# Joined two-block kernel: the start, the seams between stages and the order of the sparse attention rewritten

## The chip, the cores and the metric

One core of one Trainium2 chip. The metric is device microseconds (us) of one launch. The profile comes from one profiled execution.

## The reference, cut to what is computed

One sequence of 512 tokens, model width 1024, float32. Two blocks run one after the other.

```python
def first_block(x, c, ...):
    c_act = jax.nn.silu(c)
    for layer in range(2):
        mod = (c_act @ ada_w[layer] + ada_b[layer])[:, None, :]
        sh_a, sc_a, gt_a, sh_m, sc_m, gt_m = jnp.split(mod, 6, axis=-1)
        h = modulate(rms_norm(x, attn_norm[layer]), sh_a, sc_a)
        # layer 0: differential attention; layer 1: sparse attention
        mix = diff_attention(h, ...) if layer < 1 else nsa_attention(h, ..., *shared)
        x = x + gt_a * mix
        h = modulate(rms_norm(x, mlp_norm[layer]), sh_m, sc_m)
        x = x + gt_m * squared_relu_mlp(h, mlp_w1[layer], mlp_w2[layer])
        if layer == 0:
            h_kv = modulate(rms_norm(x, kv_norm), sh_kv, sc_kv)
            shared = nsa_shared_kv(h_kv, w_kv, cmp_pos, cmp_w1, cmp_w2)
    return rms_norm(x, final_norm)
```

The sparse attention has 16 heads in 4 groups and three branches: attention over 31 compressed keys, over selected blocks of keys, and over a window. Their outputs are weighted by gates and added. With 512 tokens the selection takes every block and the window every earlier key, so both are causal attention with a relative bias. The second block is an mLSTM layer, a dilated window attention layer and a gated addition behind each.

## The kernel before

**Numbers.** Every large product is float32 split in two parts (`hi` on ACT writes the rounded part `wH`, `lo` on DVE the rest `wL`), and `three` (L420) issues three matmuls for it: L422, L423, L424. Activations are split in the same way into `hH` and `hL` (`apply_dve`, `apply_act`; semaphores `h_hi`, `h_lo`). A fp32 matmul that is not split shows as two instructions in the trace (x8 for four of them).

**Weights.** They come in halves of 1 MB in the order of a list. SP's `load_half(n)` waits until half n-2 is split (`w_lo`), and one half feeds 48 matmuls of 512 columns on PE. Besides, rows of the modulation weights (`ada`, 512 KB each) are loaded, and DVE reduces each with the broadcast silu(c) (`ada_sum`, L647). They go through two buffers, `adab`.

**Order.** Each engine runs a list written by hand: `pe_first`, `act_first`, `dve_first`, `sp_first` for layer 0, then `_second` for layer 1's attention and so on. Within an engine everything runs in that order. All waits are semaphores.

**The start.** SP loads c, x, the first 16 ada rows in four pieces, and the first two halves. silu(c) is an exponential on ACT and three DVE steps, one a reciprocal (L1266). Then DVE takes the sums of squares, the 16 reductions, `lo(0)`, `lo(1)` and the eight chunks of `hL`; PE's first tile waits for `h_lo`.

**A seam.** Between stages stands an RMS norm: residual and squares, one or two fp32 matmuls with a constant matrix (`stats_pe`, L512 and L515; `stats_two_pe` ahead of the second block), rstd on ACT (logarithm, exponential), then chunk by chunk `tmp` (DVE L532), `hH` (ACT L568), `hL` (DVE L541). PE's next tile waits for the first `h_lo`.

**The stage of compressed keys.** `cmp_pe` (16 x 2 products of 124 columns) runs twice between tiles 26, 27 and 28. The first waits until ACT has copied the four banks of tile 26, and ACT splits a half of weights ahead of these copies.

**Sparse attention** (`nsa_pe`, `nsa_dve`, `nsa_act`). The work is a list of units, `UNITS`. Block i has 128 queries and (i+1)*128 keys; a unit is one bank: four heads for i=0, two for i=1, one for i=2 and 3. Blocks run in the order 0, 1, 2, 3. For a unit, PE computes scores (L1525 and L1526), DVE adds the bias and takes the maximum (L1626), ACT takes the exponentials (L1730), PE transposes (L1535), ACT copies (L1737), PE multiplies with the values, 65 columns (L1564), and per branch DVE divides, gates and adds (L1639 to L1661). For each block come ahead of its units the scores over compressed keys, 32 matmuls of 32 columns (`c_scores`, L1581 and L1582), with their softmax on DVE and ACT into `sc`, transposes (L1589) and a copy into `ptc`. `tail` turns the block's output (L1599) and splits it for tile 29.

The loop of `nsa_pe`, condensed:

The loop of `nsa_pe`, condensed:

```python
for u in range(-6, UN + 5):
    if u == FIRST[i] - 6: c_scores(i)
    scores(u + 2); values(u - 2); turn(u)
    if u == FIRST[i] - 2: c_turn(i)
    if u == FIRST[i + 1] + 4: tail(i)
```

**Late in the second block** SP writes `vD` to memory, waits, and reads it back in another order (L2947 to L2949), ahead of a load of weights (half `N_K2 + 6`).

## Time and profile before

| | us |
|---|---|
| median of 3 runs | 2116.03 (2113.04 to 2121.13) |
| the profiled execution | 2119.31 |
| its span, first to last instruction | 2117.5 |
| PE busy in the span | 1979.0 (93%) |
| DVE busy | 1173.3 (55%) |
| ACT busy | 847.5 (40%) |
| mean granted TensorE clock | 0.958 |

Busy time is what an engine executed. The granted clock is 1.0 where TensorE runs at 2.4 GHz and 0.5 where it runs at 1.2 GHz, and a mean between them says what share of a stretch ran at which. In a timeline row the first number is the start from the span's beginning, the second the time covered, and the brackets hold the idle time of that engine just before, with what ended it.

### The profile page before, as it was taken

The numbers are of one execution on the slowest core, as the hardware profiler recorded it, in microseconds if no ns is written. First come the engines' busy times: TensorE is split into PE (matmuls) and PEld (weight loads), VectorE is DVE, ScalarE is ACT, GpSimd is POOL, SyncE is SP. The second block draws the span as 40 slices with busy tenths as digits, with TensorE's granted clock in tenths as the row PEclk, the third lists the DMA queues.
The fourth block names the chain that finished last, engine by engine and source line by source line (L and its number), as shares of the span: only waits on it lengthen the run. The fifth ranks groups of instructions, "written<-read, shape, count | busy, mean of one in ns | idle before, by whom it ended". The sixth has DMA issues, their size and how long they took to land.

```text
span 2117.5 us, 24340 instructions
## 1 busy us (share of the span) xinstructions
PE 1979.0 (93%) x9300; PEld 1632.0 (77%) x9300; DVE 1173.3 (55%) x2049; ACT 847.5 (40%) x1319; POOL 0.2 (0%) x4
## 2 busy tenths in 40 slices
PE   1999989999998999889989999999999999999999
PEld 0877667888886887789977888888787877777877
DVE  8557846665657465556545333435663455755554
ACT  3226723232223533356633231323444444657343
POOL 0000000000000000000000000000000000000000
PEclk9999998999999979589999999999999999999999
DMA  9661053546554222000022222222121232232021
GB/s 355 209 208 41 1 198 140 202 177 216 179 198 159 99 80 80 0 1 2 1 85 86 92 90 97 99 99 99 60 100 60 80 125 79 81 120 80 1 90 60
DMA packets 42216, 223.85 MB, mean 106 GB/s; under 512 B 4444, under 2 KB 5212, under 8 KB 23694
## 3 DMA queue, kind: packets, MB, share of 16 engines
q1 hardware_dynamic: 41602, 222.25, 29.5%
q8 instruction: 56, 0.92, 0.2%
q10 hardware_dynamic: 524, 0.41, 0.1%
q14 instruction: 34, 0.28, 0.0%
HBM read 219.45 MB, written 3.19 MB: 105 GB/s over the span
## 4 chain that ended last, share of the span: by engine, by line
PE 82%; DVE 8%; DMA 4%; ACT 4%; issue 2%; SPq 0%; DVEq 0%; ACTq 0%
PE bank L422 22%; PE bank L423 22%; PE bank L424 22%; PE bank L1564 3%; PE bank L1535 2%; DMA raw<-wts_d 2%; PE bank L1525 1%; DMA adab<-ada_d 1%; ACT wH L403 1%; PE bank L1526 1%; PE bank L2736 1%; DVE wL L408 1%; DMA ada<-ada_d 1%; DVE tmp L532 1%; PE bank L741 1%
## 5 line engine op out<-in xcount | busy, mean ns | idle before, releaser
L422 PE MATMUL bank<-hH,wH 128*128 128x512 f32 x1328 | 530.2, 399 | 59.5 <-DVE hL L541 37.0
L423 PE MATMUL bank<-hL,wH 128*128 128x512 f32 x1328 | 524.8, 395 | 0.0
L424 PE MATMUL bank<-hH,wL 128*128 128x512 f32 x1328 | 524.2, 395 | 0.0
L422 PEld LDWEIGHTS bank<-hH,wH 128*128 128x128 f32 x1328 | 254.7, 192 | 120.8 <-issue 59.3
L1006 ACT ACTIVATE wH<-raw 128x2048 fp32r<-128x2048 f32 x64 | 122.7, 1917 | 468.8 <-PE bank L424 468.8
L408 DVE TENSOR_TENSOR wL<-raw,wH 128x2048 fp32r<-128x2048 f32 x76 | 174.0, 2290 | 228.0 <-ACT wH L403 227.7
L423 PEld LDWEIGHTS bank<-hL,wH 128*128 128x128 f32 x1328 | 254.7, 192 | 53.7 <-issue 1.0
L424 PEld LDWEIGHTS bank<-hH,wL 128*128 128x128 f32 x1328 | 254.2, 191 | 54.1
L1050 DVE TENSOR_TENSOR wL<-raw,wH 128x2048 fp32r<-128x2048 f32 x64 | 146.5, 2289 | 225.8 <-ACT wH L1006 225.8
L403 ACT ACTIVATE wH<-raw 128x2048 fp32r<-128x2048 f32 x76 | 145.3, 1911 | 246.8 <-PE bank L424 208.4
L422 PE MATMUL bank<-aH,wH 128*128 128x512 f32 x512 | 199.2, 389 | 0.0
L423 PE MATMUL bank<-aL,wH 128*128 128x512 f32 x512 | 199.2, 389 | 0.0
L424 PE MATMUL bank<-aH,wL 128*128 128x512 f32 x512 | 199.2, 389 | 0.0
L647 DVE CUSTOM_DVE_ANT_0 adab<-adab,cb 128x1024 f32<-128x1024 f32 x96 | 115.4, 1222 | 90.3 <-DMA adab<-ada_d 90.3
L422 PE MATMUL bank<-wH,hH 128*128 128x512 f32 x304 | 126.0, 414 | 2.4 <-ACT kT L1239 1.7
L424 PE MATMUL bank<-wH,hL 128*128 128x512 f32 x304 | 119.9, 395 | 0.0
L423 PE MATMUL bank<-wL,hH 128*128 128x512 f32 x304 | 119.7, 394 | 0.0
L423 PEld LDWEIGHTS bank<-aL,wH 128*128 128x128 f32 x512 | 96.1, 188 | 20.0
L422 PEld LDWEIGHTS bank<-aH,wH 128*128 128x128 f32 x512 | 96.1, 188 | 19.9
L424 PEld LDWEIGHTS bank<-aH,wL 128*128 128x128 f32 x512 | 96.1, 188 | 19.9
L1564 PEld LDWEIGHTS bank<-vB,ptB 128*128 128x128 f32 x640 | 91.1, 208 | 18.2 <-issue 5.7
L1626 DVE CUSTOM_DVE_ANT_0 sB<-bank,bt 128x128 f32<-128x128 f32 (+3 forms) x128 | 59.3, 488 | 77.8 <-PE bank L1526 76.8
(367 smaller groups left out, 2633.4 us busy)
## 6 DMA issues: line engine op xcount, KB each, us to landing
raw<-wts_d SPq DMA_DIRECT2D x140, 1024.0 KB, 4.9
adab<-ada_d SPq DMA_DIRECT2D x96, 512.0 KB, 4.4
ada<-ada_d SPq DMA_DIRECT2D x4, 2048.0 KB, 22.4
bt<-bias_rows SPq DMA_DIRECT2D x1, 4096.0 KB, 13.0
x<-x_d SPq DMA_DIRECT2D x1, 2048.0 KB, 9.8
peF<-ple_d SPq DMA_DIRECT2D x2, 1024.0 KB, 5.6
out_d<-x SPq DMA_DIRECT2D x4, 512.0 KB, 2.7
pF<-p_d SPq DMA_DIRECT2D x2, 512.0 KB, 3.5
```

The costliest lines, as they stand in the source:

```text
L403: act.activation(wH[:, n % 2, :], raw[:, n % 2, :], ACT.Copy).then_inc(w_hi, 1)
L408: dve.tensor_tensor(wL[:, n % 2, :], raw[:, n % 2, :], wH[:, n % 2, :].bitcast(F32), ALU.subtract).then_inc(w_lo, 1)
L422: pe.matmul(o, l[0], r[0], start=start, stop=False)
L423: pe.matmul(o, l[0], r[1], start=False, stop=False)
L424: return pe.matmul(o, l[1], r[0], start=False, stop=stop)
L532: dve.scalar_tensor_tensor(out=tmp[:, nth(p, c) % 3, :], in0=x[:, c, :], scalar=scale(c), in1=rstd[:, :], op0=ALU.mult, op1=ALU.mult).then ...
L647: return dve.tensor_tensor_reduce(slot, slot, sb["cb"][:, :], 1.0, 0.0, ALU.mult, ALU.add, dst)
L1006: act.activation(wH[:, n % 2, :], raw[:, n % 2, :], ACT.Copy).then_inc(w_hi, 1)
L1050: dve.tensor_tensor(wL[:, n % 2, :], raw[:, n % 2, :], wH[:, n % 2, :].bitcast(F32), ALU.subtract).then_inc(w_lo, 1)
L1535: last = pe.transpose(bank[:, 2 + u % 2, j * P:(j + 1) * P], pB[:, u % 2, j * P:(j + 1) * P], ident[:, :])
L1564: last = pe.matmul(o[:, r * (HD + 1):(r + 1) * (HD + 1)], ptB[:, u % 2, part.start + j * P:part.start + (j + 1) * P], vB[:, j, b * GRP + g ...
L1626: dve.tensor_tensor_reduce(sB[:, u % 2, part], bank[:, u % 2, part], sb["bt"][:, 4 * g + r, T - w:T], -SCALE, BIG, ALU.add, ALU.min, nm[:, ...
```

## The change

1. **Start.** SP loads the column parameters first, then c, ada rows 8 to 11, x, rows 0 to 3, halves 0 and 1, rows 12 to 15 and 4 to 7. silu(c) is a sigmoid and one product. The 16 reductions take bias and gain in the same instruction and are made in two parts of eight; after the first part the chunks 0 to 3 of `hH`, `hL` are made. PE works the first four halves in the order (tile 0, half 0), (tile 1, half 0), (tile 0, half 1), (tile 1, half 1), and the halves are stored in that order. The bias table `bt` is loaded later, behind half 4.
2. **ada rows** go through four buffers. Halves 14 and 15 are loaded ahead of the reload of silu(c), and small tables behind halves 16 and 17.
3. **Seams.** `first_chunk` issues the eight matmuls of chunk 0 that need only `hH`, then waits for `h_lo`. It is used at the start, tiles 24 and 47, both MLPs and the gated additions. `fill` issues matmuls of the identity with itself into a bank that the next tile overwrites: 13 behind `stats_pe` of norms 1 to 3, 8 behind `stats_two_pe`, 10 at the start, 3, 5, 12, 9 and 3 around the sparse attention.
4. **Compressed keys.** The first `cmp_pe` waits for two banks only, and ACT copies tile 26 before it splits the next half; in `gelu_act` of the second, the copies come before the next split.
5. **Sparse attention.** Blocks 3 and 0 take turns group by group, then blocks 2 and 1. The first score matmul of block 0 covers 256 columns where the bank allows (the next matmul overwrites what is too much), and the first of each pair over compressed keys covers 160 instead of 32, for which `kcH` is stored twice. Compressed weights lie in two buffers `sc` and are turned in place; `ptc` is gone.
6. **vD** goes to memory and back two halves later.

```diff
+        def first_chunk(pe, b0, w, count):
+            pe.wait_ge(h_hi, count)
+            for m in range(4):
+                pe.matmul(bank[:, b0 + m, :], w(m)[0], hH[:, 0, :], start=True, stop=False)
+                pe.matmul(bank[:, b0 + m, :], w(m)[1], hH[:, 0, :], start=False, stop=False)
+            pe.wait_ge(h_lo, count)
+            for m in range(4):
+                pe.matmul(bank[:, b0 + m, :], w(m)[0], hL[:, 0, :], start=False, stop=False)
...
+                ahead = a in (24, 47) and j == 0
+                if ahead:
+                    first_chunk(pe, 4 * (a % 2), lambda m: wpart(n0 % 2, 0, m * P, P), hbase + 1)
+                for kk in range(1 if ahead else 0, 4):
...
+        def fill(pe, o, n):
+            for _ in range(n):
+                pe.matmul(o[:, 0:P], ident[:, :], ident[:, :], start=True, stop=True)
...
+            if s in (1, 2, 3):
+                fill(pe, bank[:, 4 * (next_a % 2) + 3, :], 13)
...
+        def ada_slot(j):
+            return sb["adab"][:, j % 4, :] if j % 4 < 3 else sb["adac"][:, :]
...
+            sp.dma_start(cols[:, :], d["cols"]).then_inc(cols_in, 16)
             sp.dma_start(sb["cb"][:, :], d["c"].to_broadcast([P, D])).then_inc(cb_back, 16)
-            sp.dma_start(x[:, :, :], d["x"]).then_inc(x_in, 16)
-            for g in range(4):
-                sp.dma_start(sb[f"ada{g // 2}"][:, 4 * (g % 2):4 * (g % 2) + 4, :],
-                             d["ada"][4 * g:4 * g + 4].rearrange("k p n -> p k n")).then_inc(ada_h[g], 16)
-                if g == 3:
-                    sp.wait_ge(ada_h[1], 16)
-                    load_half(sp, 0)
-                    sp.wait_ge(ada_h[2], 16)
-                    load_half(sp, 1)
-            sp.wait_ge(ada_h[3], 16)
+            for e in range(2):
+                for t in (1, 0):
+                    sp.dma_start(sb[f"ada{t}"][:, 4 * e:4 * e + 4, :],
+                                 d["ada"][8 * t + 4 * e:8 * t + 4 * e + 4].rearrange("k p n -> p k n"))\
+                        .then_inc(ada_in[2 * e + 1 - t], 16)
+                    if (e, t) == (0, 1):
+                        sp.dma_start(x[:, :, :], d["x"]).then_inc(x_in, 16)
+                    if (e, t) == (0, 0):
+                        load_half(sp, 0)
+                        load_half(sp, 1)
+            load_half(sp, 2)
             sp.wait_ge(f_row, 2)
             sp.dma_start(fscr, sb["frow"][:, :]).then_inc(f_out, 16)
-            sp.wait_ge(f_out, 16)
-
+            sp.wait_ge(cb_ready, 1)
...
+                if n >= 1:
+                    load_half(sp, n + 2)
                 for k in range(max(3 * n - 1, 0), min(3 * n + 2, 24)):
                     ada_load(sp, 16 + k)
+                if n == 2:
+                    sp.wait_ge(f_out, 16)
+                    sp.wait_ge(ada_pre, 16)
+                    sp.dma_start(sb["bt"][:, :, :], skewed).then_inc(bt_in, 16)
+            load_half(sp, 14)
+            load_half(sp, 15)
             sp.wait_ge(c_saved, 16)
             sp.wait_ge(y_lo, 8)
             sp.dma_start(sb["cb"][:, :], csave.to_broadcast([P, D])).then_inc(cb_back, 16)
+            for n in (16, 17):
+                for k in range(4):
+                    ada_load(sp, 40 + 4 * (n - 16) + k)
+                load_half(sp, n)
...
+            hi(act, 0)
+            act.wait_ge(ada_pre, 8)
+            apply_act(act, 0, lambda c: mod(c), chunks=range(0, 4))
+            hi(act, 1)
...
-            hi(act, 1)
-            act.wait_ge(mod_ready, 2)
-            apply_act(act, 0, lambda c: mod(c))
+            hi(act, 2)
+            act.wait_ge(ada_pre, 16)
+            apply_act(act, 0, lambda c: mod(c), chunks=range(4, KC))
...
             dve.wait_ge(cb_ready, 2)
-            dve.tensor_tensor(cb, cb, ce, ALU.mult).then_inc(cb_ready, 1)
-            dve.wait_ge(cb_ready, 3)
-            sq_dve(dve, 0, range(1, 7))
-            for g in range(4):
-                if g == 3:
-                    dve.wait_ge(par_in, 80)
+            for e in range(2):
+                for t in (1, 0):
+                    if (e, t) == (0, 0):
+                        sq_dve(dve, 0, range(1, 7))
+                    dve.wait_ge(ada_in[2 * e + 1 - t], 16)
+                    for c in range(4 * e, 4 * e + 4):
+                        a = sb[f"ada{t}"][:, c, :]
...
+
+            dve.wait_ge(ada_used, 24)
+            mod_cols(dve, 16, 24, 0)
+            mod_scale(dve, 32, ("mlp_norm", 0))
...
+            pe.wait_ge(w_hi, 1)
+            fill(pe, bank[:, 3, :], 10)
+            for n, (a, j) in enumerate(((0, 0), (1, 0), (0, 1), (1, 1))):
+                if n == 1:
+
+                    pe.wait_ge(f_row, 2)
+                pe.wait_ge(w_lo, n + 1)
+                if n == 0:
+                    first_chunk(pe, 0, lambda m: wpart(0, 0, m * P, P), 1)
...
-                pe.wait_ge(acc_free[0], 4 * 14)
+
+                pe.wait_ge(acc_free[0], 4 * 13 + 2)
...
+        GROUPS = [(i, g) for g in range(GRP) for i in (3, 0)]
+        GROUPS += [(2, 0), (2, 1), (1, 0), (1, 1), (2, 2), (1, 2), (2, 3), (1, 3)]
+        ORDER = (3, 0, 2, 1)
...
+        BEGIN = [FIRST[3, 0] - 6, FIRST[0, 0] - 6, FIRST[2, 0] - 6, FIRST[1, 0] - 10]
+        TURN = [LAST[i] + 5 for i in ORDER]
...
-                pe.wait_ge(ks_lo, i + 1)
+
+                pe.wait_ge(ks_lo, max(i + 1, 2))
                 for n, part, c, b, r in parts(u):
-                    pe.matmul(bank[:, u % 2, part], q_stack(4 * g + r, i), ksH[:, b, g, 0:w], start=True, stop=False)
+                    more = min(part.stop + P, T) if i == 0 else part.stop
+                    pe.matmul(bank[:, u % 2, part.start:more], q_stack(4 * g + r, i),
+                              ksH[:, b, g, 0:more - part.start], start=True, stop=False)
...
+            def c_scores(k):
+                i = ORDER[k]
+                if k == 0:
                     pe.wait_ge(acc_free[1], 4 * 14)
                     pe.wait_ge(acc_free[0], 4 * 15)
+                    fill(pe, bank[:, 0, :], 5)
+                    pe.wait_ge(kc_ev, 1)
...
+                    pe.matmul(bank[:, 6 + hd % 2, (hd // 2) * 32:(hd // 2) * 32 + 160], q_stack(hd, i),
+                              sb["kcH"][:, :, :].rearrange("p r n -> p (r n)")[:, g * 32:g * 32 + 160],
+                              start=True, stop=False)
...
+            def c_turn(k):
+                if k == 0:
+                    fill(pe, bank[:, 3, :], 12)
...
+            def c_copy(k):
+                act.wait_ge(x_t, k + 1)
+                act.activation(comp_flat(k), bank[:, 6, :], ACT.Copy).then_inc(x_pt, 1)
...
-                hi(act, n + 3)
+                if a < 26:
+                    hi(act, n + 3)
...
-                    hi(act, N_B1 + 1)
-                    gelu_act(act, 1, N_B1)
+                    gelu_act(act, 1, N_B1, lambda e: hi(e, N_B1 + 1))
...
+                if j == 0:
+                    first_chunk(pe, 4, lambda m: wpart(n % 2, 0, m * P, P), hbase + 1)
+                for kk in range(1 if j == 0 else 0, 4):
...
-                if n == N_K2 + 6:
+                if n == N_K2 + 8:
```

**PE at the entry of the sparse attention.** In these rows `ident` alone is `fill`, `kcH` and `kcL` are compressed keys, `ksH` and `ksL` the keys of both branches, `qs` queries, `pB` a unit's weights that are turned, `sc` compressed weights. Before:

```order
L1581 MATMUL bank<-kcH,qs_105 128x32
L1582 MATMUL bank<-kcL,qs_105 128x32
L1525 MATMUL bank<-ksH,qs_104 128x128
L1526 MATMUL bank<-ksL,qs_104 128x128
L1525 MATMUL bank<-ksH,qs_104 128x128
L1526 MATMUL bank<-ksL,qs_104 128x128
L1525 MATMUL bank<-ksH,qs_104 128x128
L1526 MATMUL bank<-ksL,qs_104 128x128
L1525 MATMUL bank<-ksH,qs_104 128x128
L1526 MATMUL bank<-ksL,qs_104 128x128
L1589 MATMUL bank<-ident,sc 128x128 x4
```

and after the change:

```order
L1668 MATMUL bank<-kcH,qs_106 128x160
L1671 MATMUL bank<-kcL,qs_106 128x32
L1606 MATMUL bank<-ksH,qs_105 128x512
L1608 MATMUL bank<-ksL,qs_105 128x512
L524 MATMUL bank<-ident 128x128 x12
L1680 MATMUL bank<-ident,sc 128x128 x4
L1606 MATMUL bank<-ksH,qs_105 128x512
L1608 MATMUL bank<-ksL,qs_105 128x512
```

The first units behind the compressed scores are of block 3 (512 columns), where they were of block 0 (128), and twelve `fill` matmuls stand ahead of the first turn. A little later, where block 3 hands over to block 0, the change has (`vB` and `ptB` are values and turned weights)

```order
L1606 MATMUL bank<-ksH,qs_105 128x512
L1608 MATMUL bank<-ksL,qs_105 128x512
L1647 MATMUL bank<-vB,ptB 128x65 x4
L1617 MATMUL bank<-ident,pB 128x128 x4
L1606 MATMUL bank<-ksH,qs_105 128x256
L1608 MATMUL bank<-ksL,qs_105 128x128
```

so units of 512 columns and of four times 128 stand side by side.

**SP at the start**, with the loads of c, x, the first ada rows, the weights and the table `bt`. Before:

```order
L1174 DMA cb<-c_d 128x1024
L1175 DMA x<-x_d 128x4096
L1177 DMA ada_63<-ada_d 128x4x1024 x2
L1177 DMA ada_64<-ada_d 128x4x1024 x2
L665 DMA raw<-wts_d 128x2048 x2
L1186 DMA bias_rows<-frow 16x640
L1190 DMA bt<-bias_rows 128x16x512
```

and after the change:

```order
L1206 DMA cb<-c_d 128x1024
L1209 DMA ada_64<-ada_d 128x4x1024
L1213 DMA x<-x_d 128x4096
L1209 DMA ada_63<-ada_d 128x4x1024
L695 DMA raw<-wts_d 128x2048 x2
L1209 DMA ada_64<-ada_d 128x4x1024
L1209 DMA ada_63<-ada_d 128x4x1024
L695 DMA raw<-wts_d 128x2048
```

The weights stand between the two parts of the ada rows, and `bt` comes eleven rows further down.

## Rows read from the trace of the kernel before

**Rows 1.** The page: granted clock of TensorE in 40 slices, in tenths.
```profile
PEclk9999998999999979589999999999999999999999
```

**Rows 2.** Windows of plain matmuls and of norm 2: us, busy (count) per engine, PEclk, DMA.
```profile
400.00:500.00 100.00, 100.00 (x443) 82.81 (x442) 57.03 (x71) 25.30 (x25) 0.00 (x0) 1.00 0.53 185
684.00:692.00 8.00, 6.64 (x17) 5.26 (x18) 7.86 (x11) 5.78 (x8) 0.00 (x0) 0.57 0.01 2
```

**Rows 3.** Timeline of PE, first matmul of the first tile.
```profile
49.97 0.77 PE L422 MATMUL bank<-hH,wH 128*128 128x512 f32 x1 [23.91 <-DVE hL L541]
```

**Rows 4.** Chain that ended last, 22 to 40 us: start, us, what.
```profile
22.33 13.39 DMA raw<-wts_d
...
35.75 1.92 ACT wH L403
...
37.69 2.29 DVE wL L408
```

**Rows 5.** Timeline of ACT and DVE at the start: x has landed, statistics, rstd.
```profile
11.05 1.67 ACT L495 ACTIVATE tmp<-x 128x512 f32<-128x512 f32 x3 [4.42 <-DMA x<-x_d]
...
15.24 4.67 DVE L503 TENSOR_TENSOR tmp<-tmp 128x512 f32<-128x512 f32 x6
...
24.57 0.63 ACT L522 ACTIVATE rstd<-rstd 128x512 f32<-128x512 f32 x1
```

**Rows 6.** Timeline of PE: idle before the diff attention and at norm 1.
```profile
151.33 0.70 PE L741 MATMUL bank<-kT,qT 64*128 64x128 f32 x4 [3.03 <-DVE nm L811]
...
317.91 2.04 PE L512 MATMUL bank<-tmp,mean 128*128 128x512 f32 x2 [4.14 <-DVE tmp L503]
...
326.04 0.77 PE L422 MATMUL bank<-hH,wH 128*128 128x512 f32 x1 [4.38 <-DVE hL L541]
```

**Rows 7.** Waits of PE, 280 to 330 us: in total, times, longest us.
```profile
PE bank L422 <- DVE wL L408: 3.8, 2, 2.0
```

**Rows 8.** Groups of DVE by line, 290 to 312 us.
```profile
L647 DVE CUSTOM_DVE_ANT_0 adab<-adab,cb 128x1024 f32<-128x1024 f32 x7 | 8.5, 1223 | 6.6 <-DMA adab<-ada_d 6.6
```

**Rows 9.** Chain at norm 2.
```profile
682.47 2.08 DVE tmp L532 x3
```

**Rows 10.** Timeline of PE at norms 2 and 4 and at a gated addition.
```profile
678.62 1.10 PE L512 MATMUL bank<-tmp,mean 128*128 128x512 f32 x2 [2.49 <-DVE tmp L503]
...
685.36 0.77 PE L422 MATMUL bank<-hH,wH 128*128 128x512 f32 x1 [4.38 <-DVE hL L541]
...
1491.71 0.76 PE L422 MATMUL bank<-hH,wH 128*128 128x512 f32 x1 [4.31 <-DVE hL L538]
...
1763.71 0.47 PE L422 MATMUL bank<-hH,wH 128*128 128x512 f32 x1 [1.48 <-DVE hL L538]
```

**Rows 11.** Timeline of PE: first `cmp_pe`, and tile 28 behind the second.
```profile
757.93 0.44 PE L422 MATMUL bank<-fH,wH 128*128 128x124 f32 x1 [4.20 <-issue]
...
816.08 0.80 PE L422 MATMUL bank<-hH,wH 128*128 128x512 f32 x1 [2.52 <-ACT gx L1399]
```

**Rows 12.** Windows in the sparse attention.
```profile
866.00:884.00 18.00, 16.44 (x76) 16.07 (x75) 5.96 (x37) 5.28 (x16) 0.00 (x0) 0.50 0.00 0
1006.00:1071.00 65.00, 63.64 (x501) 58.94 (x500) 35.15 (x108) 42.53 (x73) 0.00 (x0) 1.00 0.00 1
852.70:1079.20 226.50, 204.92 (x1425) 195.17 (x1425) 127.10 (x448) 117.40 (x234) 0.00 (x0) 0.84 0.00 1
```

**Rows 13.** Timeline of PE: pairs of 32 and of 256 columns at the full clock.
```profile
994.05 0.26 PE L1582 MATMUL bank<-kcL,qs 128*128 128x32 f32 x1
994.16 0.26 PE L1581 MATMUL bank<-kcH,qs 128*128 128x32 f32 x1
...
918.04 0.28 PE L1525 MATMUL bank<-ksH,qs 128*128 128x256 f32 x1
918.16 0.28 PE L1526 MATMUL bank<-ksL,qs 128*128 128x256 f32 x1
```

**Rows 14.** Timeline of PE in the second block, where `vD` is moved.
```profile
1887.90 0.77 PE L422 MATMUL bank<-hH,wH 128*128 128x512 f32 x1 [3.98 <-DVE wL L408]
```

More of the change, by code:

```diff
@@ L614, in stats_two_pe @@
             pe.matmul(both, mean, sq_slot2(7), start=False, stop=True).then_inc(stat_mm, 1)
+            fill(pe, bank[:, 7, :], 8)
         def root_act(act, s, bank_, dst, eps):
@@ L989, in mlp_pe @@
                             continue
-                        for kk in range(4):
+                        if (q, j) == (0, 0):
+                            first_chunk(pe, 4 * st, lambda m: wpart(n0 % 2, 0, m * P, P), hbase - KC + 1)
+                        for kk in range(1 if (q, j) == (0, 0) else 0, 4):
                             k = 4 * j + kk
@@ L1393, in cmp_pe, with gelu_act @@
                 last.then_inc(half_used, 1)
-        def gelu_act(act, s, n):
+        def gelu_act(act, s, n, then=None):
             act.wait_ge(half_used, n)
@@ L1401, in gelu_act @@
                                ACT.Copy).then_inc(c_ev, 1)
+            if then:
+                then(act)
             act.wait_ge(c_sq, 4 * s + 4)
@@ L1719, in nsa_dve @@
                     lo(dve, HALF0["b_out"])
-                for i in range(NT):
-                    if u == FIRST[i + 1] + 5:
-                        tail(i)
+                for k in range(NT):
+                    if u == TURN[k] + 1:
+                        tail(k)
         def nsa_act(act):
@@ L1813, in act_second @@
             act.wait_ge(c2_mm, 1)
-            act.activation(sb["kcH"][:, :], bank[:, 4, 0:P], ACT.Copy).then_inc(kc_hi, 1)
+            for r in range(2):
+                act.activation(sb["kcH"][:, r, :], bank[:, 4, 0:P], ACT.Copy).then_inc(kc_hi, 1)
             act.wait_ge(g_mm, 1)
@@ L1912, in pe_second @@
             last.then_inc(g_mm, 1)
+            fill(pe, bank[:, 7, :], 3)
             pe.wait_ge(g_e, 1)
@@ L1921, in pe_second @@
             nsa_pe(pe)
+            fill(pe, bank[:, 0, :], 3)
             pe.wait_ge(y_lo, 8 + 8)
```

325 lines of the change are left out of this document (163 added, 162 removed).

## The prediction, made before the changed kernel had run

> **What bounds the kernel now.** I read the page first. The time table has PE busy in 93% of the span, DVE in 55%, ACT in 40%, and the slices of the granted clock [rows 1] are 9 nearly everywhere and fall to 8 in the seventh and to 7, 9, 5 and 8 in the fifteenth to eighteenth, that is, in the seams around the compressed keys and in the sparse attention. So the kernel is bound by matmuls, and time can be lost in two ways: PE waits, or PE runs at 1.2 GHz. The second is dear: in the plain stretch from 400 to 500 us, 443 matmuls take 100 us at granted clock 1.00, or 0.226 us each, while at norm 2, at a mean clock of 0.57, 17 take 6.64 us [rows 2]. A matmul at the low clock costs almost double. Next come the idle times of PE in the timeline, in order of time, and at each one what ended it. Last, windows of the sparse attention with busy times beside the clock.
>
> Every sum below is made against the profiled execution, 2119.31 us, which is 3.28 above the median of 2116.03. A measurement of this kernel can tell about 0.5% (10.6 us) from no change.
>
> **Start.** PE's first tile starts at 49.97 [rows 3]. The chain ahead of it is transfers: all 8 MB of modulation rows, then the weights, landed at 35.72, then their split, 1.92 on ACT and 2.29 on DVE [rows 4], then the rest of the reductions, a second split and the first `hL`. The change puts x at fourth place and the weights ahead of half of the modulation rows. Before, x had landed at 11.05 together with c, some 2.7 MB into the queue with what followed it [rows 5]; I estimate 0.4 MB per us from 8 MB of rows and 1 MB of weights landing between 11 and 35.7. Then x is there at about 16.3, the second piece at 21.3 and half 0 at 23.8. Squares, statistics and rstd took from 11.05 to about 25.2 before, partly waiting for other work [rows 5]. Their critical part is some 11 us, so rstd stands at about 27.6, the split of half 0 at about 29.5, that of half 1 and the reductions of the second part at about 31.8. The first `hH` needs one more ACT step, 33.3. First matmul at about 33.8, **16 gained**. The later halves then just keep up: `bt` is out of their way until half 5.
>
> **The waits at the diff attention and norm 1.** PE idles 3.03 ahead of the diff attention [rows 6] and twice 2 us (3.8 in all) in tiles 6 and 7, both for `wL` on DVE [rows 7]. Behind these stand modulation rows: DVE's seven reductions in 290 to 312 us take 8.5 and wait 6.6 for their transfer [rows 8]. With four buffers in place of two the transfer is ahead of its reduction, so the splits queued behind it aren't late. I take 2.4 of the 3.03 (what is left is the diff attention's own start) and all of the **3.8**. At norm 1 PE waits 4.14 for the squares [rows 6]. Norm 2, where nothing holds DVE up, waits 2.49 [rows 10]: the difference, 1.65, goes. The fp32 statistics took 2.04 at norm 1 [rows 6] and 1.10 at norm 2 [rows 10], so at the high clock 0.9 to 1.4 go with the idle time in front: I take 1.4.
>
> **A seam.** At norm 2 the three `tmp` take 2.08 from 682.47 [rows 9], the first of them 0.7; `hH` of chunk 0 follows in 0.64, so `h_hi` stands at 683.9, `h_lo` lets PE go at 685.36 [rows 10]. `first_chunk` gains **1.4** where the eight matmuls that need only `hH` fill the time. The `fill` matmuls cost nothing while PE waits for rstd anyway: 4.38 us of idle time [rows 10] take 13 of them, 26 instructions, each bound by a 128-column weight load. I have no row of exactly this; the nearest are matmuls of 32 columns, 0.11 apart at the full clock [rows 13], so 26 take 2.9, and at the low clock, twice that, 5.7. Between 0 and 1.3 of cost per seam; I take 0, for PE comes to the norm at the full clock. What they give is the clock: PE runs 8 us at 0.57 behind norm 2 [rows 2], that is 6.9 us low, of which half, 3.4, is loss. I take 2.8 here, 3.2 at norm 1 (longer idle), 1.4 at norm 3 and 2.4 at norm 4, whose wait is the same, 4.31 [rows 10], and whose fill is shorter.
> Norm 1: 3.8 + 1.65 + 1.4 + 1.4 + 3.2 = **11.4**. Norms 2, 3, 4: 4.2 + 2.8 + 3.8 = **10.8**. Two gated additions, 1.48 idle [rows 10], 1.4 each: **2.8**. The fill only helps if the idle time is what drops the clock.
>
> **Compressed keys.** The first `cmp_pe` waits 4.20 [rows 11]. In front of it ACT splits a half (1.92 [rows 4]) and makes four copies of which only two are needed now, 1 us: up to 2.9 earlier. Tile 27 behind it is held by DVE and ACT, whose work shifts by the same and by the split: 3.9. Tile 28 behind the second waits 2.52 for `gx` [rows 11]; the copies that now come first let 0.8 of that go, and the high clock of its stretch 1.2. **5.9**, between 0 and 7.
>
> **Sparse attention.** From 852.7 to 1079.2 are 226.5 us, PE busy 204.9, at a mean clock of 0.84 [rows 12]. A mean of 0.84 between 0.5 and 1.0 is 32% of the stretch at the low level, 72.5 us, which costs 36. So the PE work at the full clock is some 169 us, and 21.6 are idle. Where is it low? From 866 to 884 PE is busy 16.44 of 18 at 0.50: units of block 0, 76 matmuls of 32 to 128 columns [rows 12]. From 1006 to 1071, with units of 512 columns, busy 63.6 of 65 at 1.00. The busy share of the two is much alike, what differs is the number of columns. So I expect the clock to follow how much is streamed. The change pairs units of block 3 with units of block 0 and widens the narrow matmuls. Widening is nearly free: pairs of 32 columns are 0.11 apart at the full clock, of 256 columns 0.12 [rows 13], both bound by their weight load; 64 matmuls from 32 to 160 and 24 from 128 to 256 cost at most 88 x 0.01 = 0.9 us, and I put 0.5. Blocks 2 and 1 together are wide enough as well. Left low: the entry, where DVE and ACT start up, and the tail, about 17 us, 8.5 of cost, by the 13 to 20 us that the twelve, nine and three `fill` do not cover. 36 − 8.5 = 27.5. Of the 21.6 idle, the last unit of a small block no longer stands alone: 4.4 go, among them the wait for tile 29. DVE is busy 127 and ACT 117 [rows 12], under the 195 that are left; the new order adds nothing to them, as the turn of compressed weights is still one copy. The wait that comes next is PE for DVE's maximum where block 3 hands to block 0. Minus the 0.5: **31.4**.
> The Trainium skill, "TensorE: Matmul & The Clock Gate", section "HAM oscillation — how this bites in real kernels", puts the loss of clock down to idle gaps of PE. By that rule 866 to 884 should be fast, widening would do nothing, and the total would be that of rival 1; the row speaks against it.
>
> **vD.** PE waits 3.98 for the half queued behind the read-back [rows 14]. Two halves later the read-back is still ahead of its use: 4.0, and 2.4 for slow matmuls behind, as at norm 4. **6.4**. What is late next is the transfer itself, if the halves are less than one buffer ahead there.
>
> **Sum:** 16 + 2.4 + 11.4 + 10.8 + 2.8 + 5.9 + 31.4 + 6.4 = 87.1. Profiled 2032.2, median **2029** us.
>
> **Rivals.**
> 1. The clock in the sparse attention falls as often as now. For it: idle gaps of PE stay, 21.6 us of them, and block 1's units are narrow in any order. Against: the busy but slow stretch [rows 12]. Then 27.5 shrinks to about 8: 2048. Chance 0.2.
> 2. The start is held by loads: half 5 behind `bt`, or reductions of the second part that delay the second split. 13.39 from modulation rows to weights [rows 4] shows that the queue is full. It gives 8 instead of 16: 2037. Chance 0.08.
> 3. The fills run at the low clock: 5.7 in place of 2.9, longer than the wait that they cover, so each of four seams loses 1.3 and its clock gain: 9.8 + 4 x 1.3 = 15, 2044. Chance 0.07.
> 4. Other side. Alternation ties PE to DVE and ACT: for every bank of 512 columns, a narrow unit's four-head exponentials stand in their queues, PE idles between groups, and the clock stays low through the whole stretch. 169 x 2 + 21.6 = 360 instead of 226.5: +133 − 55.7 (all other terms) = +77, 2193. It makes the kernel slower by 0.5% from a stretch of 226.5 + 55.7 + 10.6 = 293 us on. Against it: DVE's 127 us in a stretch of 226. Chance 0.02.
> 5. The order isn't what the text says: the rows of the order rule it out for PE and SP; 0.01 left for it or a mishap.
>
> **How the numbers follow.** The forecast has 0.62. Below it: the whole sparse attention at the full clock (8.5), idle times down by 10 more and a start at 30 (4) give 2006. Above: rivals 1 to 3 lie at 2037 to 2048, two of them together at 2060. Range 2006 to 2060. All of it is over 40 us below the median before, so faster 0.96, within 0.5% 0.02, slower 0.02.
>
> **What would show it.** First matmul at 33.8 (under 36); seam idle times in two parts around a row of fills, clock 0.9 or more in the window that was 0.57; no wait for `wL` in 280 to 330 us; the stretch of the sparse attention at 195 us and a mean clock near 0.96; no wait of 3.98 in the second block. The forecast is wrong if the clock there stays at 0.84, or if idle time grows past 22 us.

## The result, and the profile after

The median is 2042.4 us (3 runs, 2037.29 to 2045.85) against 2116.03 before: ratio 0.9646, 95% interval 0.9602 to 0.9691. Forecast was 2029, in a range of 2006 to 2060. The kernel gained 73.6 us instead of 87.1. The profiled execution took 2045.85 (span 2043.3), the one before 2119.31 (span 2117.5), so between the traces 74.2 us of span have to be found.

The page of the changed kernel, where the slices answer to [rows 1]:

```profile
PE 1966.8 (96%) x9478; PEld 1623.7 (79%) x9478; DVE 1165.3 (57%) x2046; ACT 847.5 (41%) x1321; POOL 0.2 (0%) x4
...
PE   5999899999999999998999999999999999999998
...
PEclk9999999999999978998999999999999999999999
```

PE executes 12 us less in total and waits far less. The clock still falls in slices 15 and 16 (the compressed keys and the entry of the sparse attention) and in slice 19 (the compressed scores of the last block). The mean granted clock is 0.981, before 0.958.

The timeline of PE gives the places that answer to [rows 3, 6, 10, 11, 14] (start, us covered, instruction, idle before it):

```profile
34.48 0.77 PE L432 MATMUL bank<-hH,wH 128*128 128x512 f32 x1
...
133.08 0.70 PE L771 MATMUL bank<-kT,qT 64*128 64x128 f32 x4 [1.12 <-DVE nm L841]
...
642.77 1.02 PE L533 MATMUL bank<-tmp,mean 128*128 128x512 f32 x2
644.43 1.13 PE L536 MATMUL bank<-tmp,mean 128*128 128x512 f32 x2 [0.64 <-ACT tmp L510]
645.40 3.06 PE L524 MATMUL bank<-ident 128*128 128x128 f32 x26
648.77 0.47 PE L432 MATMUL bank<-hH,wH 128*128 128x512 f32 x1 [0.31 <-ACT hH L591]
...
715.52 0.29 PE L424 MATMUL bank<-fH,wH 128*128 128x124 f32 x1 [1.22 <-issue]
...
1020.10 0.79 PE L424 MATMUL bank<-hH,wH 128*128 128x512 f32 x1
...
1427.22 0.47 PE L432 MATMUL bank<-hH,wH 128*128 128x512 f32 x1 [1.26 <-ACT hH L589]
```

Set beside the same places before, what was gained up to each and in each part:

| place | before | after | gained so far | in this part | forecast |
|---|---|---|---|---|---|
| first matmul | 49.97 | 34.48 | 15.5 | 15.5 | 16 |
| diff attention | 151.33 | 133.08 | 18.3 | 2.8 | 2.4 |
| statistics of norm 2 | 678.62 | 642.77 | 35.9 | 17.6 | 11.4 |
| first `cmp_pe` | 757.93 | 715.52 | 42.4 | 6.6 | 7.1 |
| sparse attention begins | 852.70 | 808.05 | 44.7 | 2.2 | 3.0 |
| tile 29 | 1079.18 | 1020.10 | 59.1 | 14.4 | 31.4 |
| first matmul behind norm 4 | 1491.71 | 1427.22 | 64.5 | 5.4 | 4.2 |
| end | 2117.5 | 2043.3 | 74.2 | 9.7 | 11.6 |

(The forecast's 7.1 is norm 2's 4.2 and the 2.9 of the first `cmp_pe`. The clock term of norm 4, 2.4, is booked to the part behind it.) Every part came out within 1.9 us or better than forecast but one: the sparse attention gained 14.4 in place of 31.4. Its windows, the first the whole stretch as in [rows 12], the others its low-clock parts (us, busy and count of PE, PEld, DVE, ACT, POOL, granted clock, DMA share, GB/s):

```profile
808.10:1020.10 212.00, 196.77 (x1475) 184.28 (x1474) 125.03 (x446) 117.34 (x234) 0.00 (x0) 0.93 0.00 1
808.10:820.22 12.12, 12.12 (x57) 11.93 (x57) 6.97 (x14) 0.63 (x1) 0.00 (x0) 0.50 0.00 0
827.05:833.87 6.82, 6.82 (x29) 6.25 (x28) 3.08 (x7) 0.82 (x2) 0.00 (x0) 0.50 0.00 0
932.86:943.10 10.24, 10.24 (x50) 10.24 (x49) 3.35 (x9) 0.99 (x2) 0.00 (x0) 0.50 0.00 0
1018.19:1020.10 1.91, 1.78 (x10) 1.48 (x8) 1.30 (x2) 1.89 (x3) 0.00 (x0) 0.50 0.00 0
```

Low are 31 us, where I had allowed 17. All of it but 2 us is the compressed scores of the first, second and fourth block with what stands beside them, and in these parts PE is busy without a pause. Two of them have waits just in front: PE waited 1.36 and 1.49 us at the entry, and the clock fell at 806.57, inside the `fill` that followed; it waited 2.48 us ahead of the fourth block's scores, and the clock fell 0.8 us behind that wait. Only the fall at 827.05 comes out of a busy stretch, the 6.8 us at the full clock ahead of it, with 0.33 us of idle time in all:

```profile
820.22:827.05 6.83, 6.50 (x48) 5.47 (x48) 2.24 (x8) 4.12 (x7) 0.00 (x0) 1.00 0.01 2
```

And busy time in the stretch is 196.8, where I had counted on 169.5 of work and 8.5 for the low clock.

### The profile page after: what moved, and what is told of

Read it like the earlier page. It is cut to its first block, busy times and chain, and to the rows that moved or that the text cites. A ratio compares the mean times of both kernels' runs of the same rounds, so it can differ in the third digit from the quotient of the medians.

```text
span 2043.3 us, 24682 instructions
## 1 busy us (share of the span) xinstructions
PE 1966.8 (96%) x9478; PEld 1623.7 (79%) x9478; DVE 1165.3 (57%) x2046; ACT 847.5 (41%) x1321; POOL 0.2 (0%) x4
## 4 chain that ended last, share of the span: by engine, by line
PE 85%; DVE 7%; ACT 3%; DMA 2%; issue 2%; SPq 0%; DVEq 0%; ACTq 0%
PE bank L424 23%; PE bank L425 23%; PE bank L426 23%; PE bank L1647 3%; PE bank L1617 1%; DVE wL L410 1%; PE bank L2838 1%; PE bank L1606 1%; PE bank L771 1%; PE bank L2190 1%; PE bank L1608 1%; PE bank L1668 1%; DMA x<-x_d 1%; ACT wH L405 1%; DMA adab<-ada_d 1%
## 5 line engine op out<-in xcount | busy, mean ns | idle before, releaser
L424 PE MATMUL bank<-hH,wH 128*128 128x512 f32 x1276 | 501.6, 393 | 6.4 <-DVE wL L410 4.1
L425 PE MATMUL bank<-hL,wH 128*128 128x512 f32 x1276 | 498.1, 390 | 0.0
L426 PE MATMUL bank<-hH,wL 128*128 128x512 f32 x1276 | 497.9, 390 | 0.0
L424 PEld LDWEIGHTS bank<-hH,wH 128*128 128x128 f32 x1276 | 240.5, 189 | 58.6 <-issue 6.1
L425 PEld LDWEIGHTS bank<-hL,wH 128*128 128x128 f32 x1276 | 240.6, 189 | 50.4 <-issue 1.0
L426 PEld LDWEIGHTS bank<-hH,wL 128*128 128x128 f32 x1276 | 240.5, 188 | 50.4
L1720 DVE CUSTOM_DVE_ANT_0 sB<-bank,bt 128x512 f32<-128x512 f32 (+3 forms) x128 | 59.3, 488 | 65.9 <-PE bank L1608 65.8
L1647 PEld LDWEIGHTS bank<-vB,ptB 128*128 128x128 f32 x640 | 84.3, 196 | 15.6 <-ACT ptB L1834 6.6
L671 DVE CUSTOM_DVE_ANT_0 adab<-adab,cb 128x1024 f32<-128x1024 f32 x72 | 84.8, 1219 | 16.3 <-DMA adab<-ada_d 16.3
```

Source lines behind the costliest of these rows:

```text
L424: pe.matmul(o, l[0], r[0], start=start, stop=False)
L425: pe.matmul(o, l[0], r[1], start=False, stop=False)
L426: return pe.matmul(o, l[1], r[0], start=False, stop=stop)
L671: return dve.tensor_tensor_reduce(slot, slot, sb["cb"][:, :], 1.0, 0.0, ALU.mult, ALU.add, dst)
L1647: last = pe.matmul(o[:, r * (HD + 1):(r + 1) * (HD + 1)], ptB[:, u % 2, part.start + j * P:part.start + (j + 1) * P], vB[:, j, b * GRP + g ...
L1720: dve.tensor_tensor_reduce(sB[:, u % 2, part], bank[:, u % 2, part], sb["bt"][:, 4 * g + r, T - w:T], -SCALE, BIG, ALU.add, ALU.min, nm[:, ...
```

## The experiments

All ratios are to the kernel before, on the same chip, 5 rounds; the low-clock time of a stretch is read from the clock of the profiled execution, of which there is one for each kernel. The difference of two such ratios is uncertain by about 0.003, or 6 to 7 us, so a smaller effect is read from its own place in the traces. Code lines below are condensed. First the changed kernel again, with its order, its widenings and its fills changed one by one.

**again.** 

> The changed kernel once more, as the base for the other runs on this chip. Its first profile has the sparse attention (first matmul over compressed keys to first matmul of tile 29) at 212.0 us, mean granted clock 0.93, PE idle 15.2 us in it, where the prediction had 197.5 with the clock near 0.96. Every theory: 2042 us within 5, the stretch at 210 to 214.

Measured: 2045.76 (2041.13 to 2049.80), ratio 0.9650 (0.9624 to 0.9675). Stretch 213.3, low 35.8 (the prediction's sum gives a stretch of 195.1). Between executions of this one kernel the total moves by 12 us.

**narrow.**
```
-                    more = min(part.stop + P, T) if i == 0 else part.stop
+                    more = part.stop
-   pe.matmul(bank[:, 6 + hd % 2, c:c + 160], q_stack(hd, i), kcH[:, g * 32:g * 32 + 160], ...)
+   pe.matmul(o, q_stack(hd, i), kcH[:, 0, g * 32:(g + 1) * 32], ...)
```


> Both widenings undone (160 back to 32 columns over compressed keys, 256 back to 128 for block 0). Theory A (the clock follows what is streamed, and a widened matmul costs nothing because its weight load bounds it): low-clock time in the stretch grows from 31 to about 50 us, stretch +8, total 2050. Rival B (only idle gaps of PE drop the clock; idle stays as it is): clock and time unchanged, 2042, or 1 us faster for the columns saved.

Measured: 2047.51, ratio 0.9661 (0.9638 to 0.9683). Stretch 215.1, low 37.6. The 8 us of theory A didn't show: it is 2 us by the ratio, within its uncertainty, and 2 to 3 us in the stretch.

**nofill_nsa.** The calls `fill(pe, ..., 5)`, `12`, `9` of `nsa_pe` and both `3` around it deleted.

> The five fill calls at the entry, in and behind the sparse attention taken out (5, 3, 12, 9, 3 matmuls). They stand for 11.2 us of PE in the stretch, 27 of the 48 instructions at the low clock. Theory A: most of them cover waits for DVE, so idle time takes their place (some 8 us more idle), the stretch is 0 to 3 us shorter or equal, total 2040 to 2043. Rival C (the fills pay for the missing 13 us of the forecast): stretch shorter by 8 or more, total under 2035. Rival D (they hold the clock): stretch longer by 4 or more.

Measured: 2044.64, ratio 0.9653 (0.9629 to 0.9677). Stretch 210.1, low 29.2. Theory A holds: idle time of PE in the stretch is 22.3 in place of 15.2. So without fills the new order and the widths leave as much idle time as the 21.6 us before. The fills pay for nothing and cost next to nothing, since nearly all of them stand where PE would wait.

**sequential.**
```
-        GROUPS = [(i, g) for g in range(GRP) for i in (3, 0)]
-        GROUPS += [(2, 0), (2, 1), (1, 0), (1, 1), (2, 2), (1, 2), (2, 3), (1, 3)]
-        ORDER = (3, 0, 2, 1)
+        GROUPS = [(i, g) for i in range(4) for g in range(GRP)]
+        ORDER = (0, 1, 2, 3)
```
and the waits of `c_scores` and `tail` on bank 6 as that order needs them.

> Blocks in the order 0, 1, 2, 3 again, with widening and fills kept. Theory A: the units of block 0 stand alone, PE waits for DVE between them as before (waits of 1.7 to 2.9 us), clock low through most of block 0, low time about 50 us, stretch 220 to 224, total 2052. Rival E (the order is worth nothing, the widening did it): stretch 212, total 2042.

Measured: 2044.73, ratio 0.9658 (0.9633 to 0.9683). Stretch 209.9, low 23.9. Theory A is wrong here and rival E fits: with the widenings kept, the order is worth nothing that shows. But narrow says the same of the widenings with the order kept, so one kernel was missing.

**seq_narrow.** Both edits together.

> The fourth cell of the table: blocks in the order 0, 1, 2, 3 and the widenings undone too, fills kept. Each of the two undone alone cost 2 us or nothing (stretches 215.1 and 209.9 against 212 to 213.3). Theory F (either one is enough to keep the clock up, so they stand in for each other): low-clock time of the stretch goes to 55 us or more, stretch 220 to 226, total 2055. Rival G (neither matters; what the stretch gained came from the fills and the entry): stretch 210 to 214, total 2045.

Measured: 2051.97 (2050.72 to 2058.59), ratio 0.9686 (0.9673 to 0.9699). The four stretches side by side, in the order changed kernel again, narrow, sequential, both:

```profile
809.70:1023.02 213.32, 199.10 (x1474) 186.57 (x1473) 125.21 (x446) 117.28 (x234) 0.00 (x0) 0.92 0.00 1
```
```profile
809.30:1024.36 215.06, 199.72 (x1474) 186.90 (x1473) 125.39 (x446) 117.36 (x234) 0.00 (x0) 0.91 0.00 1
```
```profile
804.66:1014.54 209.88, 191.01 (x1475) 181.55 (x1474) 125.70 (x448) 117.00 (x234) 0.00 (x0) 0.94 0.01 1
```
```profile
811.69:1031.99 220.30, 203.87 (x1475) 193.92 (x1474) 125.42 (x446) 116.96 (x234) 0.00 (x0) 0.88 0.00 1
```

Only the last has a clear loss: 53 us low, stretch 220.3. By these four profiles it is theory F: order and width do the same job and stand in for each other. This isn't shown beyond doubt. By the ratios narrow loses 2 us, sequential 2 and both together 8, each uncertain by 6 to 7, so that two losses that simply add are possible too; and the low-clock time of a stretch differs by 16 us, the wrong way, between sequential and wide_both_seq (below), which has the same order and wider matmuls. What is shown is that undoing both costs time. Of the 14.4 us between the 226.5 before and the 212.1 after, some 8 come from order and width together, and some 6 from what seq_narrow still has: fills in place of waits, and the new entry.

**nofill_seams.** `fill(..., 13)` of `stats_pe` and `fill(..., 8)` of `stats_two_pe` deleted.

> The fills behind the statistics of norms 1 to 3 (13) and of norm 4 (8) taken out, first_chunk kept. Theory (the prediction's term): behind each seam PE runs at the low clock for 3 to 7 us again, as before, 3.2 + 2.8 + 1.4 + 2.4 = 9.8 lost, total 2055. Rival (with first_chunk in front the idle time is 1.4 us shorter, so the clock holds without fills): total 2045, no low clock behind a seam.

Measured: 2051.27 (2044.63 to 2058.18), ratio 0.9674 (0.9652 to 0.9696): some 5 us lost, 9.8 expected, with a wide spread. Its own places say more. From a tile's first matmul to the next mark (the statistics, or `cmp_pe`) this kernel takes 1.6 us longer than the changed one behind norm 1, 2.9 behind norm 2 and 2.8 behind norm 3; from the first matmul behind norm 4 to that of the first gated addition it takes 1.1 or 3.3 more, by the one or the other profile of the changed kernel. That is 8 to 11 in all, where the prediction had 3.2, 2.8, 1.4 and 2.4. Norm 2 shows what a fill buys. Timeline of PE without fills:

```profile
650.08 0.76 PE L432 MATMUL bank<-hH,wH 128*128 128x512 f32 x1 [3.21 <-ACT hH L591]
```
its window of 8 us:
```profile
648.00:656.00 8.00, 5.92 (x14) 4.69 (x15) 7.49 (x11) 6.00 (x8) 0.00 (x0) 0.58 0.00 1
```
and the same window in the changed kernel, where 26 fill instructions cover the wait (above, 645.40):
```profile
648.00:656.00 8.00, 7.69 (x37) 6.31 (x36) 7.86 (x12) 6.38 (x8) 0.00 (x0) 1.00 0.00 1
```
The first matmul isn't earlier by the fill (3.80 us behind the last of the statistics in both), but 37 instructions run in the 8 us, five of them the last of the fill, where 14 did. (The tile begins 1.3 us later without fills; in a window moved by as much it has 20, at the same 0.58.) Without fills PE was low for 3 us behind norm 1, 7 behind norm 2, 7 behind norm 3 and 3 behind norm 4.

**nofirst.**
```
             pe.wait_ge(h_hi, count)
+            pe.wait_ge(h_lo, count)
```


> first_chunk waits for h_lo before its first matmul; fills kept. Theory: 1.4 us come back at each of the start, four norm seams and two gated additions, 9.8 in all, total 2055; the fills end 1.7 us before the first matmul and the clock may fall behind one or two seams, 3 more. Rival (PE is bound there by the next h_lo anyway, since chunk 1's hL comes no sooner): total 2045 to 2048.

Measured: 2056.05 (2052.83 to 2060.16), ratio 0.9712 (0.9697 to 0.9728): 10 us lost by the medians, 13 by the ratio, against 9.8 in the theory. From the last matmul of the statistics to the first of the tile are 4.96, 4.98, 4.90 and 4.90 us at the four norms, 3.79, 3.80, 3.67 and 3.64 with `first_chunk`: 1.2 each, 1.4 forecast. At the two gated additions it is 1.3 each, at the start 0.6, so 8 us in all; and the clock fell behind one seam, for 3.4 us behind norm 4. The wait that was covered by the fill comes back behind it (norm 2):

```profile
649.23 0.47 PE L433 MATMUL bank<-hH,wH 128*128 128x512 f32 x1 [1.48 <-ACT hH L592]
```
(The releaser named is ACT; the wait added is for `h_lo`, which DVE gives.)

**vd_early.** `if n == N_K2 + 8` back to `+ 6`.

> vD goes to memory and back ahead of the half it stood ahead of before. Theory (the prediction's term): PE waits 4 us for that half's wL again and runs some 7 us at the low clock behind it, total +6.4, 2052. Rival (the three earlier reasons for lateness are gone, so the load is early enough anyway): total 2045, no wait of PE over 2 us in the second block besides those that are there now.

Measured: 2050.05 (2046.93 to 2058.96), ratio 0.9688 (0.9665 to 0.9712), 8 us lost by the ratio, give or take 7; 6.4 forecast. At its own place the loss is 7.7: from the first matmul of the first gated addition to the fp32 matmuls behind this half, 133.7 us in the changed kernel (1697.11 to 1830.80), take 141.4 here. The wait is back and longer than in [rows 14], and the clock is low for 7 us (1817.57 to 1824.39), from within the wait on:

```profile
1819.61 0.77 PE L424 MATMUL bank<-hH,wH 128*128 128x512 f32 x1 [5.17 <-DVE wL L410]
```

**ada_two.**
```
             if j < 4:
                 sp.wait_ge(ada_in[j], 16)
-            else:
-                sp.wait_ge(ada_used, j - 3)
+            if j >= 2:
+                sp.wait_ge(ada_used, j - 1)
...
-                            sp.wait_ge(ada_used, g * 16 + (32 + c - 3))
+                            sp.wait_ge(ada_used, g * 16 + (32 + c - 1))
```


> The modulation rows keep their four buffers, but SP lets only two be outstanding (it waits for the reduction of the row two back). Theory: the two waits for wL in tiles 6 and 7 (2 us each), the longer wait ahead of norm 1 and the one at the diff attention come back, 3.8 + 1.65 + 2.4 and some low clock, 8 to 11 in all, total 2053 to 2056. Rival (two are enough since the loads at the start are shifted): total 2046.

Measured: 2064.81 (2056.58 to 2065.92), ratio 0.9731 (0.9713 to 0.9748). 17 us lost by the ratio, about double what I gave them. The wait at the diff attention is back, with 3.61 us. Norm 1 begins at 307.0 in place of 288.5, with 5.28 us of idle time ahead of it. Half of the loss is at a place that I had not costed, an early tile behind the load of `bt`:

```profile
97.07 0.79 PE L424 MATMUL bank<-hH,wH 128*128 128x512 f32 x1 [7.78 <-DVE wL L410]
```
DVE had waited 14.65 us for a modulation row just before (next fence): with two outstanding, the third row of a group is asked for late, and the next half of weights is queued behind it on SP.
```profile
93.58 1.23 DVE L671 CUSTOM_DVE_ANT_0 adab<-adab,cb 128x1024 f32<-128x1024 f32 x1 [14.65 <-DMA adab<-ada_d]
```
 Without four buffers the new start isn't kept: the 15.5 us are there at the first matmul (34.32) and partly gone at 97. In the changed kernel no wait there is over 1 us.

The two waits for `wL` in tiles 6 and 7 did not come back, so that the two buffers caused them isn't shown. Another one did, at norm 2:
```profile
665.08 1.10 PE L533 MATMUL bank<-tmp,mean 128*128 128x512 f32 x2 [2.67 <-DVE tmp L518]
```
It was 2.49 before [rows 10] and is absent in the changed kernel, and here DVE has waited 2.56 us for a modulation row at 655.30, as it had before (2.49 at 668.72). So the wait at norm 2 stood for modulation rows too, where the prediction took it for one that nothing on DVE lengthens.

**wide_cmp_mid.** One step beyond the change.
```
-    last = three(pe, bank[:, m, 0:124], w, (fH[:, l, :], fL[:, l, :]), l == 0, l == 15)
+    n = 248 if l < 15 else 124
+    last = three(pe, bank[:, m, 0:n], w, [f_flat[:, l * 124:l * 124 + n] for f_flat in (fH, fL)], l == 0, l == 15)
-    apply_act(act, 3, shift); hi(act, N_B0)
+    apply_act(act, 3, shift, mid=lambda e: hi(e, N_B0))
-    apply_dve(dve, 3, 2, scale, shift); lo(dve, N_B0)
+    apply_dve(dve, 3, 2, scale, shift, mid=lambda e: lo(e, N_B0))
```


> Beyond the change: the 186 of 192 matmuls of cmp_pe with 124 columns take 248 (the 124 behind them go to columns of the bank that nobody reads), and the split of tile 27's first half comes in the middle of the chunks of h instead of behind them. In the changed kernel the first cmp_pe runs dense, with no idle time, and yet falls to the low clock 2.3 us after it began and stays there for 20.5 us at 0.21 us for 124 columns. Theory A (streamed columns decide): the low stretch shrinks to 3 to 7 us, the 0.21 and 0.11 us per matmul stay as they are, tile 27 starts up to 7 us earlier, total 2036 to 2039. Rival B (idle gaps decide, there the 1.2 us in front of cmp_pe): low stretch as long, total 2045. Rival H (the engine is bound by columns too, so 248 cost double at the high clock): total 2050 or more.

Measured: 2036.87 (2035.55 to 2039.67), ratio 0.9619 (0.9606 to 0.9632). The total is theory A's; its cause isn't shown. In the first profile of the changed kernel the clock of the first `cmp_pe` falls in the middle of a dense run:

```profile
717.56 0.28 PE L424 MATMUL bank<-fH,wH 128*128 128x124 f32 x1
717.67 0.27 PE L425 MATMUL bank<-fL,wH 128*128 128x124 f32 x1
717.78 0.36 PE L426 MATMUL bank<-fH,wL 128*128 128x124 f32 x1
717.94 0.42 PE L424 MATMUL bank<-fH,wH 128*128 128x124 f32 x1
718.15 0.42 PE L425 MATMUL bank<-fL,wH 128*128 128x124 f32 x1
718.37 0.42 PE L426 MATMUL bank<-fH,wL 128*128 128x124 f32 x1
```
Starts go from 0.11 apart to 0.21. With 248 columns the same 96 matmuls stand 0.114 apart all through:

```profile
717.90 0.28 PE L425 MATMUL bank<-fL,wH 128*128 128x248 f32 x1
718.02 0.28 PE L426 MATMUL bank<-fH,wL 128*128 128x248 f32 x1
718.13 0.28 PE L424 MATMUL bank<-fH,wH 128*128 128x248 f32 x1
```
and their window:
```profile
714.30:725.40 11.10, 11.10 (x96) 10.99 (x96) 8.29 (x10) 7.35 (x9) 0.00 (x0) 1.00 0.27 96
```
The idle time in front is the same (1.22 us), and the run takes 11.1 us in place of 18.6 (715.52 to 734.1, where the trace shows the next idle time). Rival H (columns cost time) falls. Theory A and rival B aren't decided by this, for the other profile of the changed kernel (again), with 124 columns and the same wait in front, kept the full clock through all 96:

```profile
714.79 0.30 PE L424 MATMUL bank<-fH,wH 128*128 128x124 f32 x1 [1.22 <-issue]
...
725.42 0.28 PE L426 MATMUL bank<-fH,wL 128*128 128x124 f32 x1
734.01 0.77 PE L424 MATMUL bank<-hH,wH 128*128 128x512 f32 x1 [8.31 <-issue]
```

They stand 0.112 apart. Of the ten profiles with these 124-column matmuls behind this wait, three lost the clock inside the run (the changed kernel's first, nofill_nsa, sequential) and seven did not. The second `cmp_pe`, the same 96 matmuls with no wait in front, kept it in all ten and in the profile of before.

Nor does the clock of this run set the time. In all ten, tile 27 begins 19.2 us behind the first of the 96, whether PE has then waited 8.31 us, as above, or hardly at all, as in the changed kernel's first profile:
```profile
734.74 0.76 PE L424 MATMUL bank<-hH,wH 128*128 128x512 f32 x1 [0.60 <-issue]
```
In the three kernels with the split in the middle it begins 15.8 us behind:
```profile
730.05 0.76 PE L424 MATMUL bank<-hH,wH 128*128 128x512 f32 x1 [4.62 <-issue]
```
So 3.5 us of the gain are the earlier split's. The rest goes with less low clock elsewhere: 52 us in the whole profile, 80 and 86 in the two of the changed kernel, and a mean clock of 0.985 to 0.989 in its five executions against 0.979 to 0.985. Whether the columns do that or the moved split wasn't separated; the kernel with one of the two edits alone is missing.

**wide_both.** That kernel, and the second matmul of each pair over compressed keys with 160 columns too (`kcL2` stands for `kcL` stored twice).
```
-    last = pe.matmul(o, q_stack(hd, i), kcL[:, g * 32:(g + 1) * 32], start=False, stop=True)
+    last = pe.matmul(bank[:, 6 + hd % 2, c:c + 160], q_stack(hd, i), kcL2[:, g * 32:g * 32 + 160], start=False, stop=True)
```


> The last kernel (wider cmp_pe, split in the middle: 2036.9) and besides the second matmul of each pair over compressed keys with 160 columns in place of 32, for which kcL is stored twice. Theory A (streamed columns decide, weight loads bound the time): the pair stays at 0.22 us at the high and 0.43 at the low clock, the low-clock times around 815 and 921 us of that kernel's trace (17 us) shrink by 7 to 10 us, total 2033. Rival B (idle gaps decide): 2037. Rival H (160 columns behind 160 are no longer hidden): pairs of 0.25 us or more, total 2038.

Measured: 2038.05 (2033.93 to 2039.02), ratio 0.9607 (0.9594 to 0.9620). A pair takes 0.224 us at the full clock and, in the two that run at the low one, some 0.43; before it was 0.223 and 0.427, so rival H is out. The stretch is 206.6 with 14.6 low, 208.8 with 20.3 in the kernel ahead:

```profile
805.87:1012.51 206.64, 189.11 (x1474) 176.80 (x1473) 124.81 (x446) 117.36 (x234) 0.00 (x0) 0.96 0.01 1
```
By the total it can't be told from wide_cmp_mid (their intervals overlap), so theory A's 2033 against 2037 stays undecided.

**wide_both_seq.** The same in the order 0, 1, 2, 3.

> The same with the blocks in the order 0, 1, 2, 3. Theory F (width and order stand in for each other): the same time within 3 us, 2030 to 2036. Rival (alternation is needed once the rest is gone): 2040 or more.

Measured: 2038.74 (2036.37 to 2044.67), ratio 0.9619 (0.9602 to 0.9636). The same within the error, though 2038.74 lies between the 2036 of theory F and the 2040 of its rival. And the profiled execution had a stretch of 214.3 with 40 us low, where sequential with narrower matmuls had 24. That neither theory A nor F explains.

## Why the prediction was right, and where it wasn't

**Right.** The start (15.5 of 16), the diff attention (2.8 of 2.4), the seams and vD came as worked out, each by its own mechanism: `first_chunk` is worth 8 us at its seven places (seven at 1.4 made 9.8), the fills hold the clock behind a norm (8 to 11 us for 9.8), vD's wait of 4 us and the low clock behind it are both real (7.7 at its place, 6.4 forecast).

**The four buffers** were under-costed. The term had the waits that the trace of before showed, 2.4 + 3.8 + 1.65. The run ada_two puts all of it at 17, and half of that stands early, where with the new start the rows of modulation weights and `bt` meet the first halves. The old trace didn't hold this cost; that its later first matmul hid it is my reading, not shown. The part from the diff attention to norm 2 gained 17.6 where 11.4 was forecast, and two things explain the surplus. The waits for the squares went whole at norm 1 and at norm 2, 4.14 and 2.49, where 1.65 was booked: the prediction read norm 2's wait as one where "nothing holds DVE up", but DVE had stood 2.49 and 0.76 us for modulation rows ahead of it, and ada_two brings the wait back. That is 5.0. And 31 us were low before, 22.4 of them busy, against 10 and 8.4 now, so the clock gave 7.0 in place of 4.6. These two are 7.4, of which 1.2 are lost again in the rest of the part.

**The sparse attention** is the step that failed: 31.4 forecast, 14.4 measured. That the clock would be held was right in direction, its size wrong, in two terms; that widening and mixing together hold part of it is borne out by seq_narrow, and which of them does it isn't shown.
- *The clock term*, "36 − 8.5 = 27.5". Half of all the low time was booked as loss, though PE stood idle in some of it, and idle time doesn't shrink with the clock. In the 72.9 us low before, PE was busy 64.6, for example

```profile
852.70:892.82 40.12, 35.28 (x162) 34.55 (x162) 18.82 (x83) 11.22 (x31) 0.00 (x0) 0.50 0.00 1
```
  so the loss was 32.3. And left low were not 17 but 31 us, all busy, 15.5. Gained were 16.8, 10.7 less than forecast. The entry and the tail, for which the 17 stood, were low for 14. The other 17 are what the sum lacked: the compressed scores of the second and the fourth block (192 columns in a pair of 0.43 us) and the wider matmuls behind them, dense once the clock is low.
- *The work*, "169 us at the full clock, and 0.5". By the right sum (busy less half of the busy low time) it was 172.6 before and 181.3 after, 8.7 more. The fill instructions in the stretch are 5.2 of it at the full clock, and the run without fills has 175.9. By the same sum narrow has 181.1, sequential 179.7 and seq_narrow 178.9, so the widening costs up to 0.8, as forecast, and the order some 2, where the forecast had nothing; about 1 us stays open. These fills replace idle time, so they bring back what they cost: idle fell by 6.4, from 21.6 to 15.2. I had 4.4 of it from the order. It took both: idle are 22.3 with the new order and no fills, and 18.9 with the fills and the old order (sequential).
- −10.7 − 8.2 + 2 = −16.9, against a miss of 17.0.

**Rivals.** The first (the clock falls as often as before, 2048) was half true in size; of its causes, idle gaps and narrow units, the runs settle neither. The Trainium skill, "TensorE: Matmul & The Clock Gate", section "HAM oscillation — how this bites in real kernels", ties the loss to idle gaps. That they are one cause is shown by norm 2 without fills. Against gaps as the only one stands the fall at 827.05, with 0.33 us of idle time in the 6.8 us ahead of it; again has the same fall, at 828.50, with the same 0.33. The first `cmp_pe` speaks for neither side: behind the same wait of 1.22 us the same kernel lost the clock in one execution and kept it in another, and without a wait in front (the second `cmp_pe`) these matmuls lost it in none of eleven profiles. Rivals 2 and 3 (loads at the start, fills at the low clock) didn't come: the fill at norm 2 took 3.06 for 26 instructions, 2.9 forecast. (In the sparse attention's entry the twelve did run at the low clock, 24 instructions in 4.91 us.) Rival 4, a stretch of 293 us or more, was far off: DVE is busy 125 of 212.

**What I gave the order** isn't borne out. The prediction told of alternation as the main cure. sequential shows that with the widths kept it brings nothing that can be measured. Only with both undone does the stretch lose 8 us; that either alone is enough fits the four profiles and isn't shown beyond their spread.

## What to carry to other kernels

Before half of a low-clock stretch is booked as loss, take its idle time out: only busy time halves. Small matmuls can take more columns for almost nothing where the surplus isn't read (0.112 us with 124 columns, 0.114 with 248); whether that holds the clock has to be seen in more than one execution, for one and the same run of matmuls kept it or lost it. A slow run of matmuls costs nothing where the next tile waits for something else: look at when the next tile begins, not at how long the run took. Two cures of one loss need not add, and a term that rests on waits seen before is too small where another edit moves the load that they stood for: undo each alone, and both, before you say which one it was.

## What was not expected

The granted clock of one and the same kernel differs between executions: low were 79.6 us in one profile of the changed kernel and 86.3 in the other, at other places (175 to 179 us in the one, 125 to 129 in the other; 16 us of the first `cmp_pe` in the one, none in the other), with totals from 2037.3 to 2049.8. The first matmul was 0.6 us earlier in the second (33.84 for 34.48); whether that shifted them isn't shown. An effect under some 6 us can't be read from these totals, only from its own place in the trace. Whether the 24 and 40 us of low clock in the two sequential kernels with wide matmuls are such a shift, or have a cause, stays open.

The fastest version tried is wide_cmp_mid or wide_both, at a ratio of 0.962 and 0.961 to the kernel before, 7 to 9 us below the changed kernel by these ratios (0.9650).
